# Even-mixer gate projections issued in pieces, a router on token rows, and two reordered spots in one long fused kernel

## The reference, cut to what matters

```python
# first block, even mixer: sliding-window attention (8 heads of 64) and retention (4 heads of 128)
y = concatenate([ya * silu(ag), yb * silu(bg)]) @ w_out      # ag, bg: gate projections of the normed x
# retention: o = intra-chunk + cross-chunk terms, then  o * rsqrt(mean(o*o) + eps)
# second block
merged = (sigmoid(g0) * (y_pool @ w_br_pool) + sigmoid(g1) * (y_mla @ w_br_mla)
          + sigmoid(g2) * (y_mem @ w_br_mem))                 # y_pool: trailing means over 2, 4, 8, 16 tokens
x = x + merged @ w_out
h2 = rms_norm(x, ffn_norm)
# router: softmax over 4 groups, the best group, the best 2 of its 8 experts, two weights per token
x = x + sum over the 2 chosen of 32 experts of  w * (silu(h2 @ w_gate) * (h2 @ w_up)) @ w_down
```

## Time and profile before

| | |
|---|---|
| time, median of 3 runs | 1814.65 us (1811.97 to 1818.83) |
| the profiled execution | 1815.36 us, of which the span is 1813.6 us |
| PE busy | 1705.8 us, 94% of the span, 7818 matmuls |
| DVE, ACT, POOL busy | 863.4, 575.7, 542.4 us |
| mean granted clock of PE | 0.968 of full |

### The profile page before, as it was taken

How to read it: one execution, slowest core, us unless ns; L and a number is a source line. 1 busy time by engine, 2 the same in 40 slices (tenths; PEclk the granted TensorE clock), 3 DMA queues, 4 the chain that set the end, 5 groups by cost and what they waited for, 6 DMA issues and landing times.

```text
span 1813.6 us, 20753 instructions
## 1 busy us (share of the span) xinstructions
PE 1705.8 (94%) x7818; PEld 1272.0 (70%) x7818; DVE 863.4 (48%) x1438; ACT 575.7 (32%) x948; POOL 542.4 (30%) x228
## 2 busy tenths in 40 slices
PE   6998899999999999999998999989899969999996
PEld 4877667887888888887875668878677745556552
DVE  4428467215644466435666724542423363433335
ACT  4116445324322244334424333232322221122112
POOL 3431114741444445732430224464323400000000
PEclk8999899999999999999999999999989969999998
DMA  4221112531322224521220113243212448888871
GB/s 157 93 78 39 56 61 84 169 108 47 100 93 93 94 83 127 162 81 49 86 77 24 58 59 94 92 131 102 70 57 90 163 162 316 332 338 339 340 279 47
DMA packets 50627, 228.08 MB, mean 126 GB/s; under 512 B 6000, under 2 KB 6896, under 8 KB 45936
## 3 DMA queue, kind: packets, MB, share of 16 engines
q1 hardware_dynamic: 48816, 222.08, 35.1%
q10 hardware_dynamic: 1728, 4.87, 0.8%
HBM read 224.82 MB, written 2.10 MB: 125 GB/s over the span
## 4 chain that ended last, share of the span: by engine, by line
issue 49%; PE 31%; POOL 16%; DVE 2%; POOLq 1%; ACT 0%; DVEq 0%; ACTq 0%
PE G L1557 19%; POOL lo_ring L478 16%; PE S L1557 4%; PE TR L1557 3%; PE O L1557 3%; PE G L2062 0%; PE TR L1651 0%; DVE U L1548 0%; POOLq L475 0%; DVE U L1416 0%; DVE sumsq L1485 0%; POOLq L477 0%; PE G L1989 0%; DVE mx L947 0%; PE TR L2036 0%
## 5 line engine op out<-in xcount | busy, mean ns | idle before, releaser
L478 POOL TENSOR_TENSOR lo_ring<-w_ring,hi_ring 128x1024 fp32r<-128x1024 f32 x222 | 541.9, 2442 | 905.2 <-ACT hi_ring L497 904.8
L497 ACT ACTIVATE hi_ring<-w_ring 128x1024 fp32r<-128x1024 f32 x222 | 234.4, 1058 | 703.9 <-PE G L1557 701.4
L1557 PE MATMUL G<-xa_hi,hi_ring 128*128 128x512 f32 x928 | 375.7, 405 | 20.3 <-POOL lo_ring L478 12.1
L1557 PE MATMUL G<-xa_lo,hi_ring 128*128 128x512 f32 x928 | 369.5, 398 | 0.0
L1557 PE MATMUL G<-xa_hi,lo_ring 128*128 128x512 f32 x928 | 369.4, 398 | 0.0
L1557 PEld LDWEIGHTS G<-xa_hi,hi_ring 128*128 128x128 f32 x928 | 176.6, 190 | 70.1 <-issue 22.4
L1557 PEld LDWEIGHTS G<-xa_lo,hi_ring 128*128 128x128 f32 x928 | 176.7, 190 | 42.6 <-issue 1.5
L1557 PEld LDWEIGHTS G<-xa_hi,lo_ring 128*128 128x128 f32 x928 | 176.5, 190 | 42.1
L1557 PE MATMUL G<-yb_hi,hi_ring 128*128 128x512 f32 x388 | 155.0, 400 | 2.4 <-POOL lo_ring L478 1.9
L906 DVE TENSOR_TENSOR arena<-G,RB 128x512 f32<-128x512 f32 x76 | 52.3, 691 | 211.0 <-PE G L1557 210.2
L1557 PE MATMUL G<-yb_hi,lo_ring 128*128 128x512 f32 x388 | 152.5, 393 | 0.0
(11 more groups left out here) (295 smaller groups left out, 2673.5 us busy)
## 6 DMA issues: line engine op xcount, KB each, us to landing
w_ring<-in_stream_dram SPq DMA_DIRECT2D x222, 512.0 KB, 3.5
arena<-in_w_gu_dram SPq DMA_DIRECT2D x16, 2048.0 KB, 8.1
ex_rings<-in_w_dn_dram SPq DMA_DIRECT2D x40, 512.0 KB, 13.4
ex_low<-in_w_gu_dram SPq DMA_DIRECT2D x8, 2048.0 KB, 12.4
ex_rings<-in_w_gu_dram SPq DMA_DIRECT2D x8, 2048.0 KB, 12.5
arena<-in_w_dn_dram SPq DMA_DIRECT2D x16, 512.0 KB, 11.7
sq<-in_w_dn_dram SPq DMA_DIRECT2D x8, 512.0 KB, 15.0
X<-in_x_in_dram SPq DMA_DIRECT2D x8, 256.0 KB, 5.6
```

The source lines that it names most:

```text
L478: nc.gpsimd.tensor_tensor(lo_ring[:, s, :], w_ring[:, s, :], hi_ring[:, s, :], ALU.subtract).then_inc(low, 1)
L497: nc.scalar.activation(hi_ring[:, m % RING, :], w_ring[:, m % RING, :], ACT.Copy).then_inc(high, 1)
L1557: return nc.tensor.matmul(*args, **kw)
```

## The change

1. Gate tiles are issued in `piece`s of two K blocks (6 matmuls), one behind each attention unit's scores and one behind each retention step: `e_ag` 0 whole, then `e_ag` 1 to 3 and `e_bg` 0 in the attention loop, `e_bg` 1 to 3 in the loop of retention heads 0 to 2. DVE normalises unit u+1 in step u. The retention output is gated first (`ret_gate`) and multiplied by the reciprocal later; the reciprocal is cut in two halves between the decay products.
2. The `pool` units go ahead of `br_mla`; their four results get tiles of their own (`pooled`) and are split behind `br_mla`. The norm of the second memory is taken inside the last `br_mla` tiles.
3. The first six rows of `merged` are split inside the last pair of `g_mem`; `w_out` begins with six K blocks.
4. Router: `U = X * gain` is transposed to token rows beside `w_out` (`rows`), ACT copies them (`ex_raw`), and the norm is applied there as a scale by token. The broadcast of the norm is gone. The choices on DVE lose some instructions, the selection is made before the weights, and the first gather runs all high products, then all low ones.

The diff, cut to its core (`...` marks what is left out, in it too):

```diff
-    ("br_mla", 16, 16, "each"),
-    ("pool", 4, 4, "each"), ("k2", 4, 4, "each"), ("v2", 4, 2, "last"), ("pool_w", 1, 4, "each"),
+    ("pool", 4, 4, "each"), ("br_mla", 16, 16, "each"),
+    ("k2", 4, 4, "each"), ("v2", 4, 2, "last"), ("pool_w", 1, 4, "each"),
...
+        pooled = [A(1664, T), A(2176, T), A(7168, T), A(10624, T)]
...
-                if t == 0 and j:
-                    high_of((y_ready, YB["swa"] + j), e_y32[:, (j - 1) % 2, :], yb_hi[:, j - 1, :])
...
+                if t == 1 and j:
+                    high_of((y_ready, YB["swa"] + j), e_y32[:, (j - 1) % 2, :], yb_hi[:, j - 1, :])
+                if t == 2:
                     gate(ACC0["e_ag"] + j, GB["ag"] + j, e_gl, e_gs, ACT.Silu)
...
+                if h > 1:
+                    ret_high(h - 2)
                 if h:
                     ret_finish(h - 1)
...
-                if h:
-                    ret_high(h - 1)
+            ret_high(2)
             ret_finish(3)
             ret_high(3)
...
+            for g in range(4):
+                unit_done("pool", g)
             for f in range(KT):
+                if f == KT - 1:
+                    norm_root("m2", D)
...
-            norm_root("m2", D)
             for g in range(4):
-                unit_done("pool", g)
-                high_of((y_ready, YB["pooled"] + g + 1), p_y32[:, g % 2, :], yb_hi[:, g, :])
+                high_of((y_ready, YB["pooled"] + g + 1), pooled[g], yb_hi[:, g, :])
...
+                    if last and f == KT - 2:
+                        act.wait_ge(full, ACC0[stage] + 2 * f + 2)
+                        for h in range(f):
+                            merged_high(h)
                     unit_done(stage, f // 2 * 3 + 2)
...
-            act.wait_ge(full, ACC0["g_mem"] + 16)
-            for f in range(KT):
-                high_of((y_ready, YB["merged"] + f + 1), U[:, f, :], xa_hi[:, f, :])
+            for f in range(KT - 2, KT):
+                merged_high(f)
...
+            def raw_rows(f):
+                act.wait_ge(tr_full, f + 1)
+                src = (O[:, :], TR[:, :])[f % 2].rearrange("p (t n) -> p t n", t=TT)
+                nc.scalar.activation(ex_raw[:, :, f * P:(f + 1) * P], src, ACT.Copy).then_inc(raw_up, 1)
...
+            raw_rows(KT - 1)
+            act.wait_ge(raw_up, KT)
+            act.wait_ge(rc_known, 1)
+            for t in range(TT):
+                nc.scalar.activation(tok_hi[:, t, :], ex_raw[:, t, :], ACT.Copy, scale=rc[:, t:t + 1]).then_inc(tm_hi, 1)
...
+            normalise(0, 2, P, swaP, sink=True)
             for u in range(16):
                 j, t = divmod(u, TT)
-                normalise(u, 2, P if t == 0 else 2 * P, swaP, sink=True)
+                if u + 1 < 16:
+                    normalise(u + 1, 2, P if t == TT - 1 else 2 * P, swaP, sink=True)
+                if t == 0 and j:
+                    swa_y(j - 1)
                 if u + 3 < 16:
                     swa_max(u + 3)
...
+                if t == 2 and j:
+                    swa_low(j - 1)
+            swa_y(3)
             swa_low(3)
...
+            def ret_gate(h):
+                g = GB["bg"] + h
+                dve.wait_ge(gate_done, g + 1)
+                dve.wait_ge(rsq, h + 1)
+                nc.vector.tensor_tensor(e_y32[:, h % 2, :], ret_o(h), e_gs[:, g % 2, :], ALU.mult).then_inc(gated, 1)
...
+            def ret_inverse(h, half):
+                r = slice(half * (T // 2), (half + 1) * (T // 2))
+                dve.wait_ge(rroot, h + 1)
+                note(nc.vector.reciprocal(ret_rinv[:, r], ret_root[:, r]))
...
             def ret_y(h):
-                g = GB["bg"] + h
-                dve.wait_ge(rroot, h + 1)
-                do(nc.vector.reciprocal(ret_rinv, ret_root))
-                do(nc.vector.tensor_tensor(e_y32[:, h % 2, :], ret_o(h), ret_rinv, ALU.mult))
-                dve.wait_ge(gate_done, g + 1)
-                nc.vector.tensor_tensor(e_y32[:, h % 2, :], e_y32[:, h % 2, :], e_gs[:, g % 2, :],
-                                        ALU.mult).then_inc(y_ready, 1)
+                settle()
+                dve.wait_ge(gated, h + 1)
+                nc.vector.tensor_tensor(e_y32[:, h % 2, :], e_y32[:, h % 2, :], ret_rinv, ALU.mult).then_inc(y_ready, 1)
...
+                    if jt == 0 and h:
+                        ret_gate(h - 1)
+                    if jt == 1 and h > 1:
+                        ret_y(h - 2)
+                    if jt == 2 and h > 1:
+                        ret_low(h - 2)
+                    if jt >= 2 and h:
+                        ret_inverse(h - 1, jt - 2)
+            ret_y(2)
+            ret_gate(3)
             ret_low(2)
+            for half in range(2):
+                ret_inverse(3, half)
             ret_y(3)
             ret_low(3)
...
+            norm_bc("m2", RBm)
             for g in range(4):
...
-                    norm_bc("m2", RBm)
+                low_of(pooled[g], yb_hi[:, g, :], yb_lo[:, g, :], y_low)
...
+                    if last and f == KT - 2:
+                        for h in range(f):
+                            low_of(U[:, h, :], xa_hi[:, h, :], xa_lo[:, h, :], y_low)
...
+            nc.vector.reciprocal(rc[:, :], root[:, :]).then_inc(rc_known, 1)
...
-                do(nc.vector.tensor_scalar(scratch, scratch, -64.0, 64.0, ALU.mult, ALU.add))
...
-                do(nc.vector.tensor_tensor(scratch, scratch, iota, ALU.add))
...
+                do(nc.vector.scalar_tensor_tensor(scratch, scratch, -64.0, ids[0], ALU.mult, ALU.add))
...
-                nc.vector.tensor_tensor(U[:, f, :], U[:, f, :], RB[:, :], ALU.mult).then_inc(h2_ready, 1)
             dve.wait_ge(m_ready, 1)
...
+                dve.wait_ge(tm_hi, t + 1)
+                nc.vector.scalar_tensor_tensor(tok_lo[:, t, :], ex_raw[:, t, :], rc[:, t:t + 1], tok_hi[:, t, :],
+                                               ALU.mult, ALU.subtract).then_inc(tm_lo, 1)
+
+            rows_low(0)
...
+            dve.wait_ge(tm_lo, 1)
+            select_rows(0, 0)
+            for t in range(1, TT):
+                rows_low(t)
...
+            def piece(name, i, hi, lo, ks):
+
...
+                if ks[0] == 0:
+                    unit_ready(n)
+                    bank_free(a)
+                for kk in ks:
+                    ins = three(G[:, a % BANKS, :], n, slice(kk * P, (kk + 1) * P), hi[:, kk, :], lo[:, kk, :],
+                                kk == 0, kk == KT - 1)
+                if ks[-1] == KT - 1:
+                    ins.then_inc(full, 1)
...
-            pe.wait_ge(evac, ACC0["e_bv"] + 4)
             pe.wait_ge(rb_ready, 1)
             for u in range(4):
+                pe.wait_ge(evac, ACC0["e_bv"] + u + 1)
                 swa_scores(u)
+            tile("e_ag", 0, xa_hi, xa_lo)
             for u in range(16):
-                if u % TT == 0:
-                    tile("e_ag", u // TT, xa_hi, xa_lo)
-                transposed(u, swaP, 2 if u % TT == 0 else 4)
+                j, t = divmod(u, TT)
+                transposed(u, swaP, 2 if t == 0 else 4)
                 if u + 4 < 16:
                     swa_scores(u + 4)
+                gates, i = ("e_ag", j + 1) if j < 3 else ("e_bg", 0)
+                piece(gates, i, xa_hi, xa_lo, range(2 * t, 2 * t + 2))
                 swa_values(u)
...
             def ret_sum(h):
-                bank_free(ACC0["e_bg"] + h + 2)
+                pe.wait_ge(evac, ACC0["e_bg"] + (1 if h < 3 else 4))
+                if 0 < h < 3:
+                    pe.wait_ge(rroot, h)
                 pe.wait_ge(rsq, h + 1)
                 mm(ret_sums(h), ones[:, :], sq[:, 0, :], start=True, stop=True).then_inc(rsum, 1)
...
             for h in range(4):
-                if h > 1:
-                    pe.wait_ge(rroot, h - 1)
-                tile("e_bg", h, xa_hi, xa_lo)
-                if h:
-                    ret_sum(h - 1)
-                pe.wait_ge(y_ready, (4, 4, 5, 6)[h])
+                if h < 2:
+                    pe.wait_ge(y_ready, 4)
+                else:
+                    pe.wait_ge(gated, h - 1)
...
+                    if h < 3:
+                        piece("e_bg", h + 1, xa_hi, xa_lo, range(2 * jt, 2 * jt + 2))
+                    if jt == 0 and h:
+                        ret_sum(h - 1)
             ret_sum(3)
...
+                          (lambda i: (rroot, 3)) if stage == "e_out" else None)
...
+                    if stage == "e_out" and f == 3:
+                        pe.wait_ge(rroot, 4)
...
+            for g in range(4):
+                tile("pool", g, xa_hi, xa_lo)
             for f in range(KT):
                 tile("br_mla", 2 * f, xa_hi, xa_lo)
                 tile("br_mla", 2 * f + 1, yb_hi, yb_lo,
                      ready=(lambda kk: (o_free, 16 + kk + 1)) if f == 0 else None)
-            norm_cols("m2")
-            for g in range(4):
-                tile("pool", g, xa_hi, xa_lo)
-                if g == 0:
-                    norm_bc("m2")
+                if f == KT - 2:
```

(89 more changed lines are left out.)

179 lines of the change are left out of this document (73 added, 106 removed).

## The result

The kernel after takes **1771.3 us** (median of 4 runs, 1770.7 to 1773.3) against 1815.9 (4 runs, 1812.0 to 1818.8) for the kernel before on the same chip: a ratio of 0.9757, 95% interval 0.9741 to 0.9773. The forecast was 1777.5 with a range of 1764 to 1794. The profiled execution has a span of 1769.3 us, 44.3 less than before.

The account below looks back on a forecast made before the run. PE, busy 94% of the span, was taken as the bound, so only its standstill or half clock could be won. Terms 16.8 - 4.9 + 3.7 + 6.8 + 1.4 + 13.4 = 37.2 off 1814.65 gave 1777.5 us, range 1764 to 1794.

Parts of the forecast that it names:

- Attention: First attention scores to first retention values: 69.8 us against 86.6, 16.8 won, heads at 14.9 us.
- units without a tile between them wait for DVE and ACT in turn: Attention heads: why one takes 17.3 us against 13.6 of PE; after, 1.42 us of matmuls stand in each unit.
- My sum from DVE's load: Attention head: four DVE units of 2.87 us, less 0.7, three products of 0.65, 1.65 of hold: 14.4, taken as 14.9.
- Rival 1: Attention loop stays as slow, head period 17 us; stage wins 10.5 instead of 16.8, time 1784; chance 0.17.
- Rival 4: PE falls to 1.2 GHz in the attention loop: stage 123 us against 86.6, time 1831; chance 0.03.
- Retention: Retention heads: 44.7 us against 39.8, 4.9 lost (1 to 8), last decay product behind half a reciprocal.
- values, square and sum: Last retention head: steps between the delayed product at 8.5 us and the start of e_out at 10.5 us.
- e_out: At e_out: the 1.9 us wait for POOL and about as much at half clock go, 3.7 won (0 to 4).
- Pool: Ahead of and in k2: 5.1 us open and 1.7 at half clock come back, 6.8 won (5 to 6.8).
- Merged rows: Ahead of w_out: start at 1395.8 because router tables are late next, 1.4 us won; 3.3 at half clock kept.
- Router: Last w_out tile to experts: 27.1 us against 43.4; transposes beside w_out cost 2.9; 13.4 won (9 to 15).
- Rival 2: Experts do not start sooner, weights waiting for flag late or DMA bounding the rounds; price 13.4, time 1791; chance 0.08.

Follow-up runs that it names:

- (1): Kernel after with the attention loop's gate tiles issued whole behind the scores of each head's first unit, normalising one unit ahead kept: 1772.6 us.
- (3): Also called both_undone: kernel after with attention gate tiles whole again and unit u normalised in step u: 1772.4 us.
- (6): Kernel of (3) with PE issuing the whole gate tile ahead of the first unit's transposes, as before: 1779.2 us.
- 4: Kernel after with DVE multiplying a head's attention output by its gate at the end of that head's last step: 1774.5 us.
- 5: Kernel of (3) with DVE's and ACT's order of before for the gate work: 1774.5 us.
- late_inverse: Also called (7): kernel after with both reciprocal halves behind all four decay products in the last retention head: 1766.7 us.
- (10): Kernel of late_inverse with the router's three tables asked for ahead of the g_mem units: 1763.8 us.
- pool_back: Kernel after with the pool units back between br_mla and k2, second memory's norm and own result tiles kept: 1773.3 us.
- best: Kernel after with late reciprocal, later gate tile evacuation in retention, early router tables and added matmuls around the first gather's waits: 1759.8 us, median of 5 runs.

## Why the prediction came out

**Attention: right number, wrong reason.** Forecast 69.8 us for the stage, measured 69.6; heads 14.9, measured 15.1. The step that failed is "units without a tile between them wait for DVE and ACT in turn ... after, each unit has 1.42 us of matmuls". Whole tiles give the same heads (1), and both halves of the advertised change can be taken back for 1.5 us of loop, 3.1 up to `e_out` (3). The 16.2 us behind the first scores are shown to be 8.7 for a tile that lies behind the scores and not ahead of them (6), 1.5 for pieces and normalising ahead together (3), and about 6 in before's last head, where the clock was 0.72 and is now 1.00. Gate order (2 to 4 us by 4 and 5) overlaps with these. My sum from DVE's load gave the right size, but what holds a head at 15.1 us is not shown: PE's six waits from the first head's start to the last head's end, 4.2 us in all, name ACT's copy and never DVE. Rival 1 (heads of 17) is what tile_before shows. Rival 4 did not come: the clock is 1.00 in the whole loop, with transposes in every unit.

The drain that the Trainium skill names beside a table load (ScalarE: Activation LUTs, What ACT_TABLE_LOAD costs) would by an estimate from its 1.38 us have left 6 of the 16.8 us. The trace shows none: after the change seven of the loop's eight loads are followed by their activation after 0.01 us, and the first waits for DVE.

**Retention: right mechanism, one term too small.** Loss 4.9 forecast, 7.0 measured. The openings of 1.5 us are there (1.47). The last head was summed as 10.5 us with its opening and took 11.8. Its delayed product was done 8.7 us in, forecast 8.5 (238.9 to 247.64); the step that was short is "values, square and sum", 2.0 us in the sum and 3.1 measured (to 250.70). PE comes out of its stop of 3.56 us at the lower clock there, which the sum left out. Its window in after, and in late_inverse, where the stop is 0.56:

```profile
247.70:250.70 3.00, 1.84 (x4) 1.06 (x5) 2.88 (x3) 1.23 (x2) 0.00 (x0) 0.50 0.36 79
```

```profile
244.20:246.40 2.20, 1.00 (x4) 0.60 (x5) 1.11 (x1) 1.53 (x3) 0.00 (x0) 1.00 0.62 162
```

The same steps take 2.2 us at full clock, with the same wait of 1.16 for ACT's square. The other 0.8 of the loss are spread over the first three heads. That the product stands behind the reciprocal is shown by (7).

**`e_out`: nearly the number, half the mechanism.** 3.3 us for 3.7. The wait of 1.9 for POOL is gone, as forecast, and two short waits for DVE's low parts (0.6) with it. But the half clock did not go: `e_out` ran some 3.5 us at the lower level before and after (clock 0.97 in 50.0 us, 0.96 in 46.7), now at its start, behind retention's stop.

**Pool: right number, cause in part.** 6.8 us from `k2` on, as forecast (7.3 in the table's longer stretch), but only 3.2 of it by the order to which I put the whole. `k2` runs in 11.7 us, no wait for POOL in it.

**Merged rows: right to a tenth.** I said that the router's tables would be late next and that PE would stop about 3.1 us; it stopped 3.23 us with that load's name, 1.3 us won for 1.4. (10) shows that nothing else was late. The 3.3 us lost at half clock behind the stop, which I kept in full, came to about half: the clock was 0.92 in the 21.7 us of the window, 1.7 lost.

**Router: 15.4 for 13.4.** Experts start 25.8 us behind the last `w_out` tile, forecast 27.1. The chain of waits, as in the earlier trace rows:

```profile
1429.80 1.28 ACT L523
...
1440.80 1.24 DVE yb_hi L1491
...
1442.08 9.43 PE G L1617 x64
```

The gather starts 15.6 us in, forecast 15.9. It takes 9.4 where I kept the 10.3 of before. The rest, 0.7, lies beside the `w_out` tiles, which grew by 2.3 us and not 2.9. Each of six groups of transposes costs 0.40 us (7.15 us from one router product to the next, 6.75 before), 2.4 in all; one router product more, 1.0, now stands ahead of the last tile; and about 1.4 come from less half clock at the start. That last gain belongs to the stop ahead of `w_out` and not to the router. Rival 2 did not come: the rounds stay at 38.1 us.

**What was not forecast: 7.0 us.** 3.1 at `k0`: before, PE waited there 1.37 us for a sum of squares and then ran at half clock, because two DVE instructions in a row met POOL's subtraction. The wait was for the second of them. The same two, before:

```profile
316.42 2.91 DVE L867 SCALAR_TENSOR_TENSOR xa_lo<-X,vec,xa_hi 128x512 fp32r<-128x512 f32 x1
319.25 2.91 DVE L875 TENSOR_TENSOR sumsq<-sumsq,sq 128x512 f32<-128x512 f32 x1
```

and after:

```profile
301.69 2.93 DVE L893 SCALAR_TENSOR_TENSOR xa_lo<-X,vec,xa_hi 128x512 fp32r<-128x512 f32 x1
304.54 0.68 DVE L901 TENSOR_TENSOR sumsq<-sumsq,sq 128x512 f32<-128x512 f32 x1
```

Before, POOL's subtraction began at 319.23, 0.02 us ahead of the second one, which took 2.91; after, it began at 304.55, 0.01 us behind it. None of the twelve experiments has that wait of PE. 2.2 lie at the very end (below). The others (1.4 of the first row, 1.0, -0.9 and 0.3) lie in code that is the same.

So the total was right partly by luck: 37.3 us of terms forecast as 37.2, in which retention's loss, 2.1 more than forecast, and the router's gain, 2.0 more, cancel, and some 7 us outside of them, nearly all of one sign.

## What to carry to other kernels

When PE issues independent work to cover a chain on other engines, put it behind the instruction that feeds the chain (here the next scores) and ahead of the one that reads it (the values); that place was worth 8.7 us, more than cutting the work into pieces. In a list that one engine serves in order, look at which small product stands behind a long instruction or a wait (a 0.23 us product behind 3.1 us): exchanging the two is a cheap edit (3.8 us up to `e_out` here), until the engine's own load becomes the limit. And a stop of PE can cost more than itself, where it comes back at the lower clock: 3.23 us of stop ahead of `w_out` were worth 4.7. The length of the stop alone does not tell: behind 3.17 us in pool_back the clock was 1.00, and behind the 1.37 us of before at `k0` it fell (0.72 from 322.2 to 328.2).

## What the runs showed of the hardware

Unchanged code moves by what the clock does in it. The memory attention took 30.2 to 30.4 us in eight of the thirteen profiles of after and its variants, and 31.3 to 31.8 in the other five, after's own among them, with the same waits of PE (8.0 and 8.2 us in all in these two). The windows, of both_undone and of best:

```profile
1271.30:1301.50 30.20, 22.26 (x82) 13.39 (x80) 16.50 (x44) 16.30 (x45) 2.34 (x1) 0.83 0.09 30
```

```profile
1262.90:1294.80 31.90, 23.74 (x82) 14.77 (x81) 16.55 (x44) 16.30 (x45) 2.34 (x1) 0.79 0.09 30
```

A clock of 0.79 for 0.83 loses 0.21 x 31.9 - 0.17 x 30.2 = 1.6 us: the whole difference. Likewise the first attention scores start anywhere between 132.6 and 135.2 us in the thirteen, with nothing changed ahead of them. Other stages hold still: the attention loop took 69.6 us in after and in each of the four variants that leave it and retention's opening as they are. So a difference of 1 or 2 us can be read from such a stage of one profile, and not from a whole time.

Behind DVE's last sum of squares comes a compare and branch over a block for further rounds, `with dve.If(more_rounds > 0)`, whose body does not run here. Before, DVE stood there for 2.21 us with nothing to wait for, and PE with it; in all thirteen profiles since it goes on at once. Before, then after:

```profile
1799.21 0.06 DVE L1545 MEMSET arena<- 128x1 f32 x1 [2.21 <-issue]
```

```profile
1755.00 0.06 DVE L1605 MEMSET arena<- 128x1 f32 x1
```

The instructions around it are the same in both kernels. Where the 2.2 us come from stays open; all that is shown is that the kernels differ in the instructions ahead of it.
